# Seven block products in place of eight in nine down-projection stages of a decoder step

## What is computed

```python
x = x + rms_norm(o, g_mix_post)
f = rms_norm(x, g_ffn_pre)
f = jnp.square(jax.nn.relu(f @ w_up)) @ w_down     # w_up 1024x4096, w_down 4096x1024
x = x + rms_norm(f, g_ffn_post)
```

## Time and profile before

| | |
|---|---|
| median of 3 runs | 2187.25 us (2186.93 to 2188.46) |
| the profiled execution's own time | 2184.32 us |
| its span in the profile | 2182.4 us |
| TensorE busy | 2095.6 us, 96% |
| VectorE / ScalarE / GpSimd busy | 1099.4 / 754.7 / 107.7 us |
| mean granted TensorE clock | 0.989 of full |

### The profile page before, as it was taken

How to read it: one execution, slowest core, us unless ns; L and a number is a source line. 1 busy time by engine, 2 the same in 40 slices (tenths; PEclk the granted TensorE clock), 3 DMA queues, 4 the chain that set the end, 5 groups by cost and what they waited for, 6 DMA issues and landing times.

```text
span 2182.4 us, 32665 instructions
## 1 busy us (share of the span) xinstructions
PE 2095.6 (96%) x14201; PEld 1908.3 (87%) x14201; DVE 1099.4 (50%) x1505; ACT 754.7 (35%) x1160; POOL 107.7 (5%) x190
## 2 busy tenths in 40 slices
PE   6999999996999999999999999999999999999998
PEld 5877777786799898989898899899898989999998
DVE  3687777877623333564333346523334564334344
ACT  4424232234433323443323244332323443323142
POOL 2011111110000000000000000000000000000000
PEclk9999999997999999999999999999999999999999
DMA  7854656563232333344332344533333333222221
GB/s 254 284 212 161 223 178 213 174 204 126 70 118 96 97 97 126 131 149 155 97 97 97 97 136 155 170 101 97 97 97 118 108 108 136 94 81 84 92 78 61
DMA packets 184835, 287.40 MB, mean 132 GB/s; under 512 B 5967, under 2 KB 162292, under 8 KB 176484
## 3 DMA queue, kind: packets, MB, share of 16 engines
q1 hardware_dynamic: 160868, 169.99, 24.3%
q0 software_dynamic: 22784, 114.28, 14.9%
q10 hardware_dynamic: 1040, 1.05, 0.1%
HBM read 245.01 MB, written 40.57 MB: 131 GB/s over the span
## 4 chain that ended last, share of the span: by engine, by line
PE 65%; DVE 4%; ACT 3%; DMA 2%; issue 1%; POOL 0%; ACTq 0%; POOLq 0%; DVEq 0%
PE mm L1875 21%; PE mm L1873 21%; PE mm L1874 21%; DVE w_lo L1161 1%; ACT w_hi L702 1%; DMA mixc<-mixT_scratch 1%; PE mm L1882 1%; PE mm L1881 1%; DMA x_in<-in_x_prompt 0%; ACT junk_y L1003 0%; DVE conv_s L1779 0%; DVE f_sb L1590 0%; PE tr L2111 0%; ACT square L976 0%; DVE o_sb L1524 0%
## 5 line engine op out<-in xcount | busy, mean ns | idle before, releaser
L1161 DVE TENSOR_TENSOR w_lo<-raw,w_hi 128x2048 fp32r<-128x2048 f32 x152 | 348.5, 2293 | 644.6 <-ACT w_hi L702 644.6
L1873 PE MATMUL mm<-act_hi,w_hi 128*128 128x512 f32 (+2 forms) x1728 | 631.3, 365 | 8.1 <-DVE act_lo L1204 5.3
L1875 PE MATMUL mm<-act_hi,w_lo 128*128 128x512 f32 (+2 forms) x1728 | 631.0, 365 | 0.0
L1874 PE MATMUL mm<-act_lo,w_hi 128*128 128x512 f32 (+2 forms) x1728 | 624.7, 362 | 0.0
L1873 PE MATMUL mm<-w_hi,u_hi 128*128 128x256 f32 x2048 | 567.9, 277 | 1.7 <-DVE u_lo L1568 0.9
L1874 PE MATMUL mm<-w_lo,u_hi 128*128 128x256 f32 x2048 | 565.5, 276 | 0.0
L1875 PE MATMUL mm<-w_hi,u_lo 128*128 128x256 f32 x2048 | 565.4, 276 | 0.0
L702 ACT ACTIVATE w_hi<-raw 128x2048 fp32r<-128x2048 f32 x152 | 290.8, 1913 | 559.9 <-PE mm L1875 464.1
L1873 PEld LDWEIGHTS mm<-w_hi,u_hi 128*128 128x128 f32 x2048 | 384.4, 188 | 4.2 <-DVE u_lo L1568 3.8
L1874 PEld LDWEIGHTS mm<-w_lo,u_hi 128*128 128x128 f32 x2048 | 384.5, 188 | 0.5
L1875 PEld LDWEIGHTS mm<-w_hi,u_lo 128*128 128x128 f32 x2048 | 384.4, 188 | 0.0
(11 more groups left out here) (269 smaller groups left out, 1512.8 us busy)
## 6 DMA issues: line engine op xcount, KB each, us to landing
raw<-in_w_ffn_up SPq DMA_DIRECT2D x64, 1024.0 KB, 5.3
raw<-in_w_ffn_down SPq DMA_DIRECT2D x64, 1024.0 KB, 5.2
w_hi<-whi_scratch POOLq DMA_DIRECT2D x24, 1024.0 KB, 5.2
w_lo<-wlo_scratch POOLq DMA_DIRECT2D x24, 1024.0 KB, 7.8
raw<-in_w_out SPq DMA_DIRECT2D x16, 1024.0 KB, 5.2
whi_scratch<-w_hi POOLq DMA_DIRECT2D x8, 1024.0 KB, 8.6
wlo_scratch<-w_lo POOLq DMA_DIRECT2D x8, 1024.0 KB, 10.7
mixc<-mixT_scratch POOLq DMA_DIRECT2D x16, 512.0 KB, 6.2
```

The costliest lines, as they stand in the source:

```text
L1161: DVE.tensor_tensor(w_lo[:, s, :, :], raw[:, s, :, :], w_hi[:, s, :, :].bitcast(fp32), ALU.subtract)\
L1873: PE.matmul(out, whi, xhi, start=(k == 0), stop=False)
L1874: PE.matmul(out, whi, xlo, start=False, stop=False)
L1875: return PE.matmul(out, wlo, xhi, start=False, stop=(k == K - 1))
```

## The change

For blocks 0 to 2 and quarters 0 to 2 (`seven(b, q)`, nine of sixteen down stages) the down product is taken as a 2x2 block product by Winograd's form of Strassen's scheme: rows in two halves of 256, hidden columns in even and odd groups of 128, output columns in two halves of 512. It takes 7 products of blocks in place of 8. Such a stage has two panels "W" of 2x256 output columns; each W panel is seven products of 24 matmuls (4 k x 2 row tiles x 3) with 256 columns, one PSUM bank each.

Its operands are sums of blocks, built and split anew:
- u: `a11`, `a12`, `a22` and the sums S1 to S4 (`s_sum`). In each up panel of such a quarter VectorE makes four sums and seven subtractions of 256 columns (`sums_1`, `sums_2`, `sum_4`, `sums_3`); the seven casts to hi go to ScalarE (`casts_1` to `casts_3`) in place of VectorE's one cast per bank.
- weights: `raw`, `w_hi` and `w_lo` are used in quarters (512 KB). GpSimd makes four sums of quarters in place for each W panel (`weight_sums`, `weight_sum_2`, `weight_sum_4`), eight a stage. ScalarE casts seven quarters (`part_hi`), VectorE subtracts seven (`part_lo`). SP loads four quarters for each W panel, each as its place comes free.
- results: each product is copied (quarter 0) or added (quarters 1, 2) by VectorE into one of seven sums (`w_add`), three of them in `mixc` and the row of `f2_sb` for the sample tile; in the first up panel of quarter 3, seven adds combine them into `f2_sb` (`w_result`). GpSimd's `mix_in` of the next block waits for that (`part_sum`).
- The products are multiplied in the order of `w_u`, which names for each how many of the u operands must be there; a11 comes first, S2, S4 and a22 last.
- Quarter 0's copies no longer go to ScalarE, and `y_tile` runs two tiles after each of the first two up panels.
- Some semaphores are merged (`smp_rc`, `smp_var`, `s_wpool` and others into neighbours).

```diff
+    def seven(b, q):
+        return b < NB - 1 and q < Q - 1
...
+            if seven(b, q):
+                order += [("W", b, q, p) for p in range(NP // 2)]
...
+        def raw_of_part(j, i):
+            b11, b21, b12, b22 = raw_at[j]
+            return quarter(raw, (b11, b21, b11, b12, b11, b22, b21)[i])
...
+        def wait_part(eng, j, i):
+            if i >= 4:
+                wait_bank(eng, j, i - 4)
+            elif order[j][3] == 1:
+                wait_bank(eng, j - 1, i + 3)
+            else:
+                wait_panel(eng, j - 2 + i // 2)
+        def wait_slot(eng, j):
+            if order[j - 1][0] == "W":
+                wait_bank(eng, j - 1, 4)
+            else:
+                wait_panel(eng, j - 2)
...
 SP
+                        if p == 0:
+                            sp.wait_ge(lo_ready, split_no[j - 2])
+                            (loads b11, b21)
+                            sp.wait_ge(lo_ready, split_no[j - 1])
+                            (loads b12, b22)
+                        else:
+                            (b11, b12, b21, b22, after parts 3, 4, 5, 6 of panel j - 1)
+                    elif order[j - 1][0] == "W":
+                        sp.wait_ge(lo_ready, split_no[j - 1] + 5)
...
 GpSimd, after results(b - 1)
+                for q in range(Q - 1 if b < NB - 1 else 0):
+                    for p in range(NP // 2):
+                        weight_sums(index("W", b, q, p))
+                        if (b, q, p) == (0, 0, 0):
+                            sample_out(1, conv_s)
+                        weight_sum_2(index("W", b, q, p))
+                        weight_sum_4(index("W", b, q, p))
+            def weight_sums(j):
+                pool.wait_ge(raw_full[raw_at[j][2]], 16 * no12)
+                pool.wait_ge(lo_ready, split_no[j])
+                GP.tensor_tensor(b11, b12, b11, ALU.subtract).then_inc(w_sums, 1)
+                pool.wait_ge(raw_full[raw_at[j][3]], 16 * no22)
+                pool.wait_ge(w_sums, n + 1)
+                GP.tensor_tensor(b12, b22, b12, ALU.subtract).then_inc(w_sums, 1)
+            def weight_sum_2(j):
+                pool.wait_ge(lo_ready, split_no[j] + 2)
+                GP.tensor_tensor(b11, b22, b11, ALU.subtract).then_inc(w_sums, 1)
+            def weight_sum_4(j):
+                pool.wait_ge(w_sums, n + 3)
+                GP.tensor_tensor(b21, b21, b11, ALU.subtract).then_inc(w_sums, 1)
...
 ScalarE, u_panel
+                if seven(b, q):
+                    squared_relu(j, 0)
+                    casts_1(j)              # a11, S3
+                    if p < NP - 2:
+                        split_hi(j + 2)
+                    squared_relu(j, 1)
+                    casts_2(j)              # a12, S1
+                    if p == NP - 2:
+                        part_hi(j + 2, 0)
+                        part_hi(j + 2, 1)
+                    if p == NP - 1:
+                        part_hi(j + 1, 2)
+                        part_hi(j + 1, 3)
+                    casts_3(j)              # S2, S4, a22
+                    return
...
 VectorE, u_panel
+                if seven(b, q):
+                    sums_1(j)               # S3 = a11 - a21; lo of a11, S3
+                    if p < NP - 2:
+                        split_lo(j + 2)
+                    sums_2(j)               # S1, S2; lo of a12, S1
+                    if p < NP - 1 or (b, q) == (0, 0):
+                        sum_4(j)
+                    if p < NP - 1:
+                        sums_3(j)           # lo of S2, S4, a22
+                    if p == NP - 2:
+                        part_lo(j + 2, 0)
+                        part_lo(j + 2, 1)
+                    return
+            def w_panel(j):
+                if order[j][3] == 0:
+                    part_lo(j, 2)
+                    if order[j][1:3] != (0, 0):
+                        sum_4(j - 1)
+                    part_lo(j, 3)
+                    w_add(j, 0)
+                    sums_3(j - 1)
+                    part_lo(j, 4)
+                    w_add(j, 1)
+                    w_add(j, 2)
+                    part_lo(j, 5)
...
+                else:
...
+                    w_add(j, 3)
+                    w_add(j, 4)
+                    split_lo(j + 1)
+                    w_add(j, 5)
+                    w_add(j, 6)
+                    split_lo(j + 2)
...
 VectorE, main loop
+                        if q == Q - 1 and p == 0 and b < NB - 1:
+                            w_result(b)
-                            y_tile(b - 1, p)
+                            y_tile(b - 1, 2 * p)
+                            y_tile(b - 1, 2 * p + 1)
...
 TensorE
+            w_u = [(a11_hi, a11_lo, 1), (a12_hi, a12_lo, 3), (s_hi[:, 0, :, :], s_lo[:, 0, :, :], 4),
+                   (s_hi[:, 2, :, :], s_lo[:, 2, :, :], 4), (s_hi[:, 1, :, :], s_lo[:, 1, :, :], 5),
+                   (s_hi[:, 3, :, :], s_lo[:, 3, :, :], 6), (a22_hi, a22_lo, 7)]
+            def w_products(j):
+                for i, (hi, lo, far) in enumerate(w_u):
+                    bank = take_bank(j, i)
+                    pe.wait_ge(lo_ready, split_no[j] + i)
+                    if p == 0:
+                        pe.wait_ge(u_lo_ready, u_before[j - 1] + far)
+                    for h in range(2):
+                        for k in range(K // 2):
+                            PE.matmul(out, hi[:, k, t], whi[:, k, :], start=(k == 0), stop=False)
+                            PE.matmul(out, lo[:, k, t], whi[:, k, :], start=False, stop=False)
+                            last = PE.matmul(out, hi[:, k, t], wlo[:, k, :], start=False, stop=(k == K // 2 - 1))
+                    last.then_inc(bank_done[bank], 1)
```

More of the change, by code:

```diff
@@ L83, in hybrid_trunk_step @@
         kind, b, q, p = order[j]
+        if kind == "W":
+            for i in range(NS7):
+                bank = (turn - 2 * NP + 4) % NRING
+                turn += 1
+                wrote[bank] += 1
+                bank_of[j, i] = (bank, wrote[bank], freed[bank])
+                freed[bank] += 1
+            bank_of[j, "last"] = bank_of[j, NS7 - 1]
+            continue
         n_banks = 2 * len(halves(b)) if kind == "U" else len(token_banks(b))
@@ L1133, in _ @@
                                 sample_swish()
-                    if q < Q - 1:
+                    if seven(b, q):
+                        for p in range(NP // 2):
+                            w_panel(index("W", b, q, p))
+                    elif q < Q - 1:
                         for p in range(NP):
@@ L1569, in u_parts, with block_lo, sums_1 @@
                                   ALU.subtract).then_inc(u_lo_ready, 1)
+            casts = itertools.count(1)
+            def block_lo(x, hi, lo):
+                dve.wait_ge(u_cast, next(casts))
+                DVE.tensor_tensor(lo, x, hi.bitcast(fp32), ALU.subtract).then_inc(u_lo_ready, 1)
+            def sums_1(j):
+                _, b, q, p = order[j]
+                at = u_no(b, q, 2 * p, 0)
+                even = square[:, 0, :]
+                dve.wait_ge(sq_ready, at + 1)
+                if at == 0:
+                    dve.wait_ge(out_small, 16 * OUT_SMALL)
+                if q == 0 and p == 0:
+                    dve.wait_ge(x2_out, 16 * no(b, NCH))
+                DVE.tensor_tensor(s_sum[:, 2, :], even[:, 0:2 * P], even[:, 2 * P:4 * P], ALU.subtract)                   .then_inc(u_hi_ready, 1)
+                block_lo(even[:, 0:2 * P], a11_hi[:, p, :], a11_lo[:, p, :])
+                dve.wait_ge(u_hi_ready, sums_before[j] + 1)
+                block_lo(s_sum[:, 2, :], s_hi[:, 2, p, :], s_lo[:, 2, p, :])
@@ L1576, in d_add @@
                 f2 = f2_sb[0:n, tile:tile + nt, p * PC:(p + 1) * PC]
-                if q > 0:
+                if q > 0 and not seven(b, q - 1):
                     old, _, free = bank_of[index("D", b, q - 1, p), i]
```

304 lines of the change are left out of this document (255 added, 49 removed).

## The result

| | before | after |
|---|---|---|
| median | 2187.3 us (2186.9 to 2188.5) | 2224.8 us (2222.5 to 2229.4) |
| profiled execution, its span | 2184.3, 2182.4 us | 2222.5, 2220.8 us |
| mean granted TensorE clock | 0.989 | 0.976 |

The change makes the kernel slower by 1.7%: ratio 1.0173, 95% interval 1.0155 to 1.0191. The forecast was 2160.5 us; the time lies above the top of its wider range, 2210 us.

A forecast was written before the change was run, and what follows sets the result against it. TensorE was taken to bound the kernel. 2184.3 - 49.0 + 2.4 + 7.0 + 9.0 + 3.9 = 2157.6, plus 2.9 to the median: 2160.5 us; own range 2148 to 2175, 8 in 10 2146 to 2210.

The forecast's parts named there:

- What was removed: Nine down stages each lose 48 matmuls at the old rate of 0.1133 us: 5.44 us each, together 49.0 us.
- no contention: Steady seven-product stages: GpSimd's weight sums, taken as 1.94 us each, hide behind the matmuls and cost nothing; chance 0.42.
- the exclusion: VectorE operations with two SBUF inputs and GpSimd's weight sums shut each other out: 4.6 us a stage, 2202 us; chance 0.34.
- Its mark: Signs of mutual blocking: VectorE's quarters at 2 to 3 us in place of 1.22, product 0 late in every stage.
- The argument against it: Against mutual blocking of VectorE and GpSimd: no row shows it, as the trace never has both engines at work.
- The prediction's other sentence: With 2.25 us per GpSimd weight sum, mutual blocking would cost 7.1 us a stage, 2225 us.
- VectorE's work: VectorE is busy 30.0 of 38.1 us in a seven-product stage, and 6.9 of 11.03 in an up panel with a weight split.
- End of the stage hidden: The next up panel's weights, behind a seven-product stage, are copied and split by 17.8 us, due at 19.0: no cost.
- Sample taps, +2.4: First up stage: VectorE has 2.4 us more work ahead of the taps, lengthening TensorE's 2.6 us wait for conv_s.
- sample_conv_out, +7.0: End of the first up stage: this step precedes the split of part 2, ready at 12.4 us, due at 5.4.
- Blocks 1 and 2, 4.5 each: First up stages: VectorE's queue with result tiles and waits takes 37.7 us, due after 33.1; 9.0 us charged together.
- Clock, +3.9: Three new long stalls are each followed by a lower TensorE clock, 1.3 us lost per stall, 3.9 together.

The follow-up runs named there:

- combo1: Changed kernel with weight sums on VectorE, two weight quarters split before the sample rows' last step, and the next up panel's load in two halves; 2169.0 us.
- sums_tiny: Changed kernel with GpSimd's eight weight sums a stage over 2 columns in place of 1024, same order and waits, part of the computation left out; 2162.8 us.
- combo6: combo1 with result tiles, a weight sum and sample taps moved, and a12's lo part made ahead of sum S2 in each up panel; 2153.1 us.
- micro: VectorE and GpSimd alone in small phases, in place of the whole kernel; with both at it VectorE starts one operation every 3.28 us (1.14 alone).
- combo3: combo1 with quarter 0's copies of blocks 1 and 2 on ScalarE, result tiles spread over three up panels, and sample taps moved earlier; 2165.4 us.
- conv_late: Changed kernel with weight parts 2 and 3 of the first seven-product stage split ahead of the sample rows' last step on VectorE; 2220.8 us.

## Why the prediction was wrong

- **What was removed: right.** 432 matmuls, and a stage of 38.1 us where nothing holds it (38.17 in combo1, 38.32 in sums_tiny). The rate kept was that of the earlier trace rows; it has a second value, 4% slower, in some stages (combo6).
- **The step that failed: "no contention" as the steady state.** The prediction set the cost of GpSimd's sums beside VectorE at nothing and made the exclusion a rival at 0.34. The rival was the truth. Its mark came as written: VectorE's quarters at 2 to 3 us where a sum runs, product 0 late in eight of nine stages. The argument against it was that no row shows both engines at work. That is no evidence: it says that the trace of before can't tell, and since the Trainium skill's rule said yes, the rival should have weighed more.
- **The size of that rival was too small, and its sum was of another kind.** 4.6 us a stage were reckoned, 6.9 measured (62.0 / 9). The rival set the work of both engines against the 38.1 us of the seven-product stage. But about half of the loss is the wait for a11_lo at the stage's start (2.0 us, and 1.7 for the clock behind it). It arises in the up stage ahead, where VectorE and GpSimd together are busy for 33.7 of 48.0 us: two sums there hold just the operations that TensorE waits for next. The rival names this place as its first sign and doesn't price it. At the stage's other end three quarter splits of 2.8 to 3.1 us stand ahead of the next load. Two more terms. A sum takes 2.34 us alone (micro) and not 1.94, taken from a one-input select. And most new waits bring a stretch of half clock, which the rival left out. Between the spans of the changed kernel and of sums_tiny lie 59.7 us: 44.1 are waits (77.8 - 33.7), 20.9 clock (53.3 - 32.4; sums_tiny has 0.985). The 5 us over can be the slower pace, which sums_tiny has in five stages and the changed kernel in one and parts of two. The prediction's other sentence, with an estimate of 2.25 us a sum from the 4497 ns for 2048 columns in the Trainium skill (GPSIMD Engine Reference, Elementwise side-by-side), gave 2225 us, and 2224.8 were measured. The duration was almost right (2.34); the time is luck, since the clock was left out, VectorE's own work was put some 2 us a stage too high, and the loss came by waits in two places and not by a full stage.
- **VectorE's work was too high, the other way.** The prediction has 30.0 us for a seven-product stage, and 6.9 for an up panel with a full split (27.6 for four, though only two of four have one); sums_tiny shows 27.7, and 23.5 for the up stage. Part of it is that instructions that follow one another overlap by 0.08 us: 1.22 recorded is 1.14 in a row (micro, 6 in 6.9 us). With the 256-column ones, 0.42 and 0.34, it is a fifth.
- **End of the stage hidden: right without contention, wrong with it.** In sums_tiny the next up panel's w_lo costs 4.0 us in all; in the changed kernel 25.6 (these lines hold whole panels of all kinds).
- **Sample taps, +2.4: 5.2** (7.8 - 2.6). I counted VectorE's added work of one panel; the taps end behind two, which is about twice that. combo3 gives all of it back.
- **sample_conv_out, +7.0: 5.6, and 0.4 for a later part.** Right place, nearly the size; conv_late shows the step as its cause.
- **Blocks 1 and 2, 4.5 each: 2.6 and 2.3** without contention, 6.5 and 6.9 with it. Right place; the part of the overlap just told in the difference isn't shown.
- **Clock, +3.9: +29.3.** The price per stall was too low: the earlier trace rows end while the clock is still down (the next 1.0 us has 0.57), and 1.3 us is part of a fall that costs 1.7, as in the changed kernel (1.2 in the stretch at 790.2, and 0.5 behind it). Above all the number of falls was wrong: thirteen more than before, four of them longer, and not three.
- With no contention the terms give 2157.6 + 2.9 and sums_tiny has 2162.8: the misses nearly cancel.

## What to carry to other kernels

GpSimd is no free engine beside a VectorE that reads two SBUF operands: add the lengths of both, count a whole GpSimd operation for each VectorE operation it may meet, above all for small ones, and ask which operand stands right behind it. Spare time in the stage doesn't help an operand that is due next. Here VectorE alone did the work sooner. What cost VectorE nothing here was a GpSimd operation that only writes, and one beside a VectorE operation with an operand in PSUM. And where every stage of a full queue gets a new stall of some 2 us, reckon the clock behind it as a term of its own; here it was half as much again.

## What the hardware showed that was not expected

- The two engines alternate strictly, one operation each, at both sizes tried (3.28 us a pair for 1.14 and 2.30; 2.48 for 0.34 and 2.30).
- A GpSimd copy of one operand shuts VectorE out as well; VectorE's 1.22 becomes 2.05 where one meets it.
- Matmuls of 256 columns have two paces at full clock, 0.1133 and 0.1178 us. A step of 0.25 us at the start of a product, which the view of waits doesn't list, is in most stages followed by the slower one for up to 312 matmuls, 1.4 us a stage. Taking that step away (combo6) takes nearly all of the slower pace away. Why some stages with the step keep the faster pace (sums_tiny), and those that start half a us late (combo1) too, stays open.
